# One weight unit of the output projection passed through the ring of the input weights, two padding tiles taken out, and an output group kept in PSUM

## The chip, the core and the metric

The kernel runs on one core of one Trainium2 chip, in one launch. The metric is the device time of that core in microseconds (us). Three runs of the kernel before took 145.35, 144.41 and 146.16 us; their median, 145.35 us, is the time before.

## What is computed

One decoder layer on 256 tokens of width 1024, all in float32:

```python
h = rms_norm(x, norm_pre_g)
q_a,k_a,v_a,g_a,f_a,q_b,k_b,v_b,g_b = split(h @ w_in)      # 16 heads of 64: 8 per group
log_f = log_sigmoid(f_a + fox_forget_b)
y_a = softmax(causal(q_a k_a / 8 + F[t] - F[s])) v_a * silu(g_a)    # F = cumsum(log_f)
y_b = softmax(causal(q_b k_b / 8 - slope * (t - s))) v_b * silu(g_b)
y = concat(y_a, y_b) @ w_out
out = x + rms_norm(y, norm_post_g)
```

With 256 tokens the block-sparse group has one block, so it is plain causal attention with a distance bias.

## The kernel before, in words

**Precision.** Each float32 operand of a large product is written as a high part (rounded to the type fp32r) and a low part (the operand minus the high part), and a product is three passes: high by high, high by low, low by high. ScalarE (ACT) makes the high part of a weight unit (`unit_high`, L385), VectorE (DVE) the low part (`unit_low`, L631), and TensorE (PE) then multiplies. All engines' programs are written out by hand in order; nothing schedules them. An engine goes on only when the semaphores that it waits for have reached their counts.

**The ring of weight units.** `w_in` is cut into units of 128 x 1024 float32 (512 KB). A unit is loaded by SyncE's queue (SP) into one of four slots of `raw`; ACT and DVE write its parts into the slot of the same number in `w_hi` and `w_lo`. Unit u uses slot u % 4. There are 8 value units (0 to 7), 8 gate units (8 to 15), and then 16 that alternate between queries and keys: query 0 is unit 16, key 0 is unit 17, and so on. Three rules tie the engines together. The load of unit u waits until the low part of unit u - 4 is made (semaphore `s_lo`). The high part of unit u waits for its load and until PE has used unit u - 4 (`s_used`). PE waits for `s_lo` before unit u. PE multiplies a gate, query or key unit in 24 matmuls of 256 columns (8 tiles of the inner dimension by three passes, `column_unit`, L942).

**The output weights.** `w_out` is eight units of the same size. Units 4 to 7 pass through the ring at its end. Units 0 to 3 are loaded outside it, into two borrowed buffers (`y_parts` and `gpost_row`), and their parts go to their own tiles `wo_hi` and `wo_lo` (L389 and L706). Two padding tiles of 32 columns lie before and after `w_hi` and `w_lo`; nothing reads them, they only move the addresses of what is allocated behind them.

**Between gates and queries.** While PE multiplies gate units 4 to 7 (units 12 to 15), DVE scales each finished gate out of PSUM (`gate_product`, L695; PE's next unit but one waits for it), makes the low part of the normalised input h in two halves (`normed_low`, L701; PE needs the first half before query 0 and the second halfway through it), and makes the low parts of units 15 to 17. At the same time the decay rows of the forget gates go through a scratch in HBM and come back spread over the partitions: ACT issues that read at L467, 1 MB into `squares`. GpSimd (POOL) then adds the causal mask in four operations (`fox_bias`, L333 and L334) that read and write SBUF. ACT makes the high parts, applies SiLU to all gates (L516, which needs all eight gate products and a table load before it), and then copies each query and key out of PSUM (L508, L512).

**The row of inverse norms.** Before the last value unit PE needs 1/rms of every token along the free dimension: DVE writes two 128 x 128 diagonal matrices (L666, into the buffer `bias`), and PE multiplies them by a tile of ones (L999) in plain float32. The result is `rrow`, which all gate products use.

**The tail.** The output rows are five groups in PSUM: columns 0 to 511 and 512 to 1023 of the first 128 tokens, columns 0 to 511 of the second (group 2), and two of 256 columns (groups 3 and 4). For each, ACT squares and sums it, DVE multiplies it by `norm_post_g` (`times_g`, L897) and, when the row's norm is known, adds it to x (`residual`, L903). Group 3 is left in PSUM by `times_g`; the others are written to `y_post` in SBUF (the profile calls that buffer `h`). Of group 4 ACT scales the columns (L613) and POOL adds x (L373), and the last store waits for that.

## Time and profile before

| | us |
|---|---|
| median of three runs | 145.35 |
| the profiled execution, as timed | 144.79 |
| its span, first to last instruction | 143.0 |
| TensorE matmul busy | 134.6 (94%) |
| VectorE busy | 109.1 (76%) |
| ScalarE busy | 97.0 (68%) |
| GpSimd busy | 39.6 (28%) |

The profile is of one execution; 1.8 us of its time lie outside the span. Busy shares are averages over stages with different limits. Matmuls are pipelined, so a matmul that "took" 0.28 us may start every 0.113 us; the start times say how fast PE goes. A start time is counted from the first instruction.

### The profile page before, as it was taken

The numbers are of one execution on the slowest core, as the hardware profiler recorded it, in microseconds if no ns is written. First come the engines' busy times: TensorE is split into PE (matmuls) and PEld (weight loads), VectorE is DVE, ScalarE is ACT, GpSimd is POOL, SyncE is SP. The second block draws the span as 40 slices with busy tenths as digits, with TensorE's granted clock in tenths as the row PEclk, the third lists the DMA queues.
The fourth block names the chain that finished last, engine by engine and source line by source line (L and its number), as shares of the span: only waits on it lengthen the run. The fifth ranks groups of instructions, "written<-read, shape, count | busy, mean of one in ns | idle before, by whom it ended". The sixth has DMA issues, their size and how long they took to land.

```text
span 143.0 us, 2849 instructions
## 1 busy us (share of the span) xinstructions
PE 134.6 (94%) x1076; PEld 127.1 (89%) x1076; DVE 109.1 (76%) x224; ACT 97.0 (68%) x199; POOL 39.6 (28%) x58
## 2 busy tenths in 40 slices
PE   7889999999999999999999999999999999999920
PEld 7778999999999999999999999999998888988920
DVE  0457967899999799888898995999679825571790
ACT  4557988269955469886884977788879823341850
POOL 3522100000000088000399417040655460220002
PEclk9999999999999999999999999999999999999996
DMA  4899999789565998866467704447800000000034
GB/s 99 252 280 385 401 395 378 236 272 376 178 181 188 419 384 244 307 198 180 132 215 249 251 5 151 147 147 249 343 5 0 0 5 0 0 0 0 0 147 149
DMA packets 9725, 26.96 MB, mean 189 GB/s; under 512 B 1384, under 2 KB 2416, under 8 KB 9456
## 3 DMA queue, kind: packets, MB, share of 16 engines
q1 hardware_dynamic: 9120, 25.57, 51.7%
q10 hardware_dynamic: 592, 1.22, 2.2%
q8 instruction: 8, 0.13, 0.4%
q14 instruction: 5, 0.04, 0.1%
HBM read 25.73 MB, written 1.06 MB: 187 GB/s over the span
## 4 chain that ended last, share of the span: by engine, by line
PE 85%; DMA 4%; DVE 3%; ACT 2%; SPq 2%; issue 1%; POOLq 1%; ACTq 0%
PE bank L942 47%; PE score_banks L952 10%; PE bank L1133 7%; PE score_banks L1133 5%; PE score_banks L1038 4%; DMA raw<-in_w_units 4%; PE value_banks L952 4%; PE value_banks L1049 1%; PE value_banks L1061 1%; PE value_banks L1065 1%; PE value_banks L1050 1%; SPq L221 1%; DVE x_t L903 1%; ACT squares L600 1%; PE bank L1051 1%
## 5 line engine op out<-in xcount | busy, mean ns | idle before, releaser
L631 DVE TENSOR_TENSOR w_lo<-raw,w_hi 128x1024 fp32r<-128x1024 f32 (+1 forms) x33 | 44.7, 1358 | 4.4 <-ACT w_hi L385 4.2
L385 ACT ACTIVATE w_hi<-raw 128x1024 fp32r<-128x1024 f32 (+1 forms) x33 | 34.8, 1057 | 6.0 <-PE bank L942 3.3
L942 PE MATMUL bank<-h_hi,w_hi 128*128 128x256 f32 x128 | 35.8, 280 | 0.0
L942 PE MATMUL bank<-h_lo,w_hi 128*128 128x256 f32 x128 | 35.4, 276 | 0.0
L942 PE MATMUL bank<-h_hi,w_lo 128*128 128x256 f32 x128 | 35.4, 276 | 0.0
L942 PEld LDWEIGHTS bank<-h_hi,w_hi 128*128 128x128 f32 x128 | 24.0, 188 | 0.4
L942 PEld LDWEIGHTS bank<-h_lo,w_hi 128*128 128x128 f32 x128 | 24.0, 188 | 0.0
L942 PEld LDWEIGHTS bank<-h_hi,w_lo 128*128 128x128 f32 x128 | 24.0, 188 | 0.0
L341 POOL TENSOR_TENSOR probs<-probs,row_inv 128x256 f32<-128x256 f32 (+1 forms) x16 | 15.7, 1006 | 27.9 <-DVE row_inv L779 27.8
L942 PE MATMUL bank<-xg_hi,w_hi 128*128 128x256 f32 x64 | 17.9, 279 | 0.0
L942 PE MATMUL bank<-xg_lo,w_hi 128*128 128x256 f32 x64 | 17.8, 278 | 0.0
L942 PE MATMUL bank<-xg_hi,w_lo 128*128 128x256 f32 x64 | 17.8, 278 | 0.0
L333 POOL TENSOR_TENSOR bias<-squares,causal 128x256 f32<-128x256 f32 x4 | 6.3, 1572 | 34.7 <-DMA squares<-decay_rows_scratch 34.7
L481 ACT ACTIVATE probs<-probs,neg_max 128x128 f32<-128x128 f32 (+1 forms) x32 | 14.1, 448 | 0.6 <-DVE neg_max L772 0.6
L942 PEld LDWEIGHTS bank<-xg_hi,w_hi 128*128 128x128 f32 x64 | 12.0, 188 | 0.0
L942 PEld LDWEIGHTS bank<-xg_hi,w_lo 128*128 128x128 f32 x64 | 12.0, 188 | 0.0
L942 PEld LDWEIGHTS bank<-xg_lo,w_hi 128*128 128x128 f32 x64 | 12.0, 188 | 0.0
L952 PE MATMUL score_banks<-w_hi,xg_hi 128*128 128x512 f32 (+2 forms) x34 | 9.0, 341 | 1.2 <-ACT w_hi L415 1.1
L952 PE MATMUL score_banks<-w_lo,xg_hi 128*128 128x512 f32 (+2 forms) x34 | 8.6, 328 | 0.0
L952 PE MATMUL score_banks<-w_hi,xg_lo 128*128 128x512 f32 (+2 forms) x34 | 8.6, 328 | 0.0
L346 POOL TENSOR_TENSOR xg_lo<-y_parts,xg_hi 128x512 fp32r<-128x512 f32 x3 | 5.3, 1773 | 11.2 <-ACT xg_hi L492 11.2
L952 PEld LDWEIGHTS score_banks<-w_hi,xg_hi 128*128 128x128 f32 x34 | 5.8, 188 | 2.3 <-issue 1.1
(167 smaller groups left out, 323.2 us busy)
## 6 DMA issues: line engine op xcount, KB each, us to landing
raw<-in_w_units SPq DMA_DIRECT2D x30, 512.0 KB, 4.3
raw<-in_w_out SPq DMA_DIRECT2D x4, 512.0 KB, 3.3
h<-in_x SPq DMA_DIRECT2D x2, 512.0 KB, 7.1
y_parts<-in_w_out SPq DMA_DIRECT2D x2, 512.0 KB, 5.7
gpost_row<-in_w_out SPq DMA_DIRECT2D x2, 512.0 KB, 4.9
squares<-decay_rows_scratch ACTq DMA_DIRECT2D x1, 1024.0 KB, 5.7
x_t<-in_x SPq DMA_DIRECT2D x1, 1024.0 KB, 7.4
raw<-in_w_units SPq DMA_DIRECT2D x3, 256.0 KB, 4.2
```

The lines of the kernel that those rows point to most:

```text
L221: sp.dma_start(raw[:, u % RING, lo:hi].rearrange("p (a c) -> p a c", a=n), w_units[units, :, part][0:n].rearrange("a p c -> p a c")).then_ ...
L333: pool.tensor_tensor(bias[:, own, :], decay[:, heads, 0:P], mask, ALU.add).then_inc(s_bias, 1)
L341: pool.tensor_tensor(own, own, row_inv[:, 4 * b + t:4 * b + 4:2].unsqueeze(2).to_broadcast((P, 2, hi - lo)), ALU.mult).then_inc(s_norm, 1)
L346: pool.tensor_tensor(y[1][:, 2 * d:2 * d + 2, :], y32[:, :, :], y[0][:, 2 * d:2 * d + 2, :].bitcast(F32), ALU.subtract).then_inc(s_ylo, 1)
L385: nc.scalar.activation(w[0][:, s, 0:width], raw[:, s, 0:width], ACT.Copy).then_inc(s_hi, 1)
L481: nc.scalar.activation(own, own, ACT.Exp, bias=neg_max[:, c:c + 1], scale=-1.0, accum_out=row_sum[:, c:c + 1]).then_inc(s_exp, 1)
L600: nc.scalar.activation(junk[:, t, cols], group, ACT.Square, accum_out=out_sq[:, n:n + 1]).then_inc(s_osq, 1)
L631: nc.vector.tensor_tensor(w[1][:, s, 0:width], raw[:, s, 0:width], w[0][:, s, 0:width].bitcast(F32), ALU.subtract).then_inc(s_lo, 1)
L942: last = nc.tensor.matmul(dst, stationary(a, j), moving(b, j), start=n == 1, stop=n == count * len(PASSES))
L952: last = nc.tensor.matmul(v_banks[t][c][:, lo - first:hi - first], xg[a][:, u, t * P:(t + 1) * P], w[b][:, u % RING, lo:hi], start=u == 0 ...
L1038: last = nc.tensor.matmul(s_ps[:, 2 * (i % 2) + a, lo:hi], q[x][own, i % 4, t * P:(t + 1) * P], k[z][own, i % 2, 0:hi - lo], start=n == 0, ...
L1133: last = nc.tensor.matmul(dst, y[a][:, p, t * P:(t + 1) * P], wide, start=p == 0 and (a, b) == PASSES[0], stop=p == PAIRS - 1 and (a, b) = ...
```

## The change

Six edits, all in one diff.

1. The two padding tiles beside `w_hi` and `w_lo` are gone, so those two lie 128 bytes per partition lower.
2. Output unit 0 is now ring unit 16, in slot 0, between the gates and the queries. Its parts go straight to `wo_hi` and `wo_lo`. Query 0 becomes unit 17 in slot 1, key 0 unit 18 in slot 2, and so on: keys take even slots. Outside the ring only output units 1 to 3 are left.
3. ACT no longer makes the high part of output unit 0 before the forget gates' exponential, but after unit 15; DVE makes its low part between the products of gates 5 and 6, and makes the low parts of query 0 and key 0 one after the other after the second half of h.
4. Since the slot of query 1 is now that of gate 7, its high part waits for gate 7 (before, for gate 6).
5. The diagonal matrices are made in two parts, in the key buffers `k_hi` and `k_lo`, and PE multiplies them by ones in fp32r, in two matmuls of 256 columns. POOL writes one more tile of ones.
6. `times_g` leaves group 2 in PSUM too, and `residual` reads it from there.

```diff
-        sb("ring_shift", [P, RING_SHIFT])
         w = [sb(f"w_{n}", [P, RING, V_PITCH], F32R) for n in PARTS]
-        sb("ring_shift_back", [P, RING_SHIFT])
...
-UNITS = V_UNITS + G_UNITS + QK_UNITS
-QK_0 = V_UNITS + G_UNITS
+OUT_IN_RING = V_UNITS + G_UNITS
+QK_0 = OUT_IN_RING + 1
+UNITS = QK_0 + QK_UNITS
...
-OUT_BEHIND = (V_UNITS + 3, V_UNITS + 5, V_UNITS + 11, V_UNITS + 13)
+OUT_BEHIND = (V_UNITS + 5, V_UNITS + 11, V_UNITS + 13)
...
-                if j > 1:
-                    sp.wait_ge(s_olo, j - 1)
+                if j == 3:
+                    sp.wait_ge(s_olo, 1)
...
-            out_unit_high(0)
...
-            unit_high(0, 80, V_UNITS + 5)
+            act.wait_ge(s_raw_in[0], 80)
+            nc.scalar.activation(wo[0][:, 0, :], raw[:, 0, 0:UNIT], ACT.Copy).then_inc(s_hi, 1)
...
-                unit_high(u % RING, 16 * (u // RING + 1), u + 1 - RING)
+                used = u + 1 - RING if u - RING < OUT_IN_RING else u - RING
+                unit_high(u % RING, 16 * (u // RING + 1), used)
...
+            next_high(key_unit(0))
             next_high(query_unit(1))
...
             for t in range(TT):
-                nc.vector.tensor_scalar(diag[:, t, :], ident[:, :], rstd[:, t:t + 1], None, ALU.mult).then_inc(s_diag, 1)
+                nc.vector.tensor_scalar(diag[0][:, t, :], ident[:, :], rstd[:, t:t + 1], None, ALU.mult).then_inc(s_dhigh, 1)
+            for t in range(TT):
+                dve.wait_ge(s_dhigh, t + 1)
+                nc.vector.scalar_tensor_tensor(out=diag[1][:, t, :], in0=ident[:, :], scalar=rstd[:, t:t + 1],
+                                               in1=diag[0][:, t, :].bitcast(F32), op0=ALU.mult,
+                                               op1=ALU.subtract).then_inc(s_diag, 1)
...
-            out_unit_low(0)
             unit_low(2, 15)
             gate_product(V_UNITS + 4)
             normed_low(0)
             unit_low(3, 16)
             gate_product(V_UNITS + 5)
-            unit_low(0, 17)
+            dve.wait_ge(s_hi, OUT_IN_RING + 1)
+            nc.vector.tensor_tensor(wo[1][:, 0, :], raw[:, 0, 0:UNIT], wo[0][:, 0, :].bitcast(F32),
+                                    ALU.subtract).then_inc(s_lo, 1)
             gate_product(V_UNITS + 6)
             normed_low(1)
             unit_low(1, 18)
+            unit_low(2, 19)
             gate_product(V_UNITS + 7)
             out_unit_low(1)
...
-                kept = group if n == 3 else y_post[:, t, cols]
+                kept = group if n in KEPT_GROUPS else y_post[:, t, cols]
...
-            for t in range(TT):
-                last = nc.tensor.matmul(rrow_ps[:, t * P:(t + 1) * P], ones[:, :], diag[:, t, :], start=True, stop=True)
+            for n in range(2):
+                last = nc.tensor.matmul(rrow_ps[:, 0:SEQ], ones_parts[:, :], k[n][:, 0, :], start=n == 0, stop=n == 1)
```

**VectorE between the gates and the queries.** Before, from the product of gate 4 on; `w_lo` is the low part of a weight unit (unit 15, then query 0, then key 0), `gate` a gate product, `h_lo` a half of h:

```order
L695 TENSOR_TENSOR gate<-bank,rrow 128x256 [waits unit_used]
L701 TENSOR_TENSOR h_lo<-h,h_hi 128x1024 [waits h_hi]
L631 TENSOR_TENSOR w_lo<-raw,w_hi 128x1024 [waits unit_hi]
L695 TENSOR_TENSOR gate<-bank,rrow 128x256 [waits unit_used]
L631 TENSOR_TENSOR w_lo<-raw,w_hi 128x1024 [waits unit_hi]
L695 TENSOR_TENSOR gate<-bank,rrow 128x256 [waits unit_used]
L701 TENSOR_TENSOR h_lo<-h,h_hi 128x1024 [waits h_hi]
L631 TENSOR_TENSOR w_lo<-raw,w_hi 128x1024 [waits unit_hi]
L695 TENSOR_TENSOR gate<-bank,rrow 128x256 [waits unit_used]
```

And the same place in the changed kernel:

```order
L705 TENSOR_TENSOR gate<-bank,rrow 128x256 [waits unit_used]
L711 TENSOR_TENSOR h_lo<-h,h_hi 128x1024 [waits h_hi]
L636 TENSOR_TENSOR w_lo<-raw,w_hi 128x1024 [waits unit_hi]
L705 TENSOR_TENSOR gate<-bank,rrow 128x256 [waits unit_used]
L755 TENSOR_TENSOR wo_lo<-raw,wo_hi 128x1024 [waits unit_hi]
L705 TENSOR_TENSOR gate<-bank,rrow 128x256 [waits unit_used]
L711 TENSOR_TENSOR h_lo<-h,h_hi 128x1024 [waits h_hi]
L636 TENSOR_TENSOR w_lo<-raw,w_hi 128x1024 [waits unit_hi] x2
L705 TENSOR_TENSOR gate<-bank,rrow 128x256 [waits unit_used]
```

The low part of query 0 has moved from ahead of the product of gate 6 to behind the second half of h; its old place is output unit 0's.

**ScalarE at the same place.** Before, from the store of the decay rows to the first query:

```order
L463 DMA decay_rows_scratch<-probs 8x256 [waits decay_rows]
L385 ACTIVATE w_hi<-raw 128x1024 [waits unit_used,raw_in3]
L385 ACTIVATE w_hi<-raw 128x1024 [waits unit_used,raw_in0]
L467 DMA squares<-decay_rows_scratch 128x2048 [waits decay_stored]
L385 ACTIVATE w_hi<-raw 128x1024 [waits unit_used,raw_in1]
L385 ACTIVATE w_hi<-raw 128x1024 [waits unit_used,raw_in2,constants]
L516 ACT_TABLE_LOAD
L516 ACTIVATE gate<-gate 128x2048 [waits gate_products]
L508 ACTIVATE q_hi<-bank 128x256 [waits unit_used]
```

and changed:

```order
L465 DMA decay_rows_scratch<-probs 8x256 [waits decay_rows]
L388 ACTIVATE w_hi<-raw 128x1024 [waits unit_used,raw_in3]
L468 ACTIVATE wo_hi<-raw 128x1024 [waits raw_in0]
L470 DMA squares<-decay_rows_scratch 128x2048 [waits decay_stored]
L388 ACTIVATE w_hi<-raw 128x1024 [waits unit_used,raw_in1]
L388 ACTIVATE w_hi<-raw 128x1024 [waits unit_used,raw_in2,constants]
L388 ACTIVATE w_hi<-raw 128x1024 [waits unit_used,raw_in3]
L519 ACT_TABLE_LOAD
L519 ACTIVATE gate<-gate 128x2048 [waits gate_products]
L511 ACTIVATE q_hi<-bank 128x256 [waits unit_used]
```

Between the read of the decay rows and the table load there are now three high parts instead of two: query 0, key 0 and query 1, and the last of them waits for gate 7.

## Rows read from the trace of the kernel before

**Rows 1.** The profile's page: busy time by engine, TensorE's granted clock.

```profile
PE 134.6 (94%) x1076; PEld 127.1 (89%) x1076; DVE 109.1 (76%) x224; ACT 97.0 (68%) x199; POOL 39.6 (28%) x58
PEclk9999999999999999999999999999999999999996
```

**Rows 2.** The chain that ended last: shares, then two pieces (start, us, what).

```profile
PE 85%; DMA 4%; DVE 3%; ACT 2%; SPq 2%; issue 1%; POOLq 1%; ACTq 0%
...
26.43 0.45 PE bank L999 x4
...
41.14 24.60 PE bank L942 x216
```

**Rows 3.** L942 by stretch: length, PE busy, PEld busy, clock, DMA share, GB/s.

```profile
35.22:38.04 2.82, 2.82 (x27) 2.82 (x25) 1.00 0.45 151
38.04:40.76 2.72, 2.72 (x26) 2.69 (x24) 1.00 0.64 208
51.98:54.70 2.72, 2.72 (x26) 2.72 (x25) 1.00 0.91 318
```

**Rows 4.** Timeline of PE: start, us, operation, [idle before <-releaser].

```profile
10.29 0.38 PE L952 MATMUL score_banks<-w_hi,xg_hi 128*128 128x256 f32 x1 [0.44 <-ACT w_hi L415]
...
26.15 0.28 PE L952 MATMUL value_banks<-w_lo,xg_hi 128*128 128x264 f32 x1
26.27 0.61 PE L999 MATMUL bank<-bias,ones 128*128 128x128 f32 x4
26.63 0.48 PE L952 MATMUL score_banks<-w_hi,xg_hi 128*128 128x512 f32 x1
```

**Rows 5.** Timeline of DVE at the diagonal matrices.

```profile
23.65 0.48 DVE L666 TENSOR_SCALAR bias<-ident,rstd 128x128 f32<-128x128 f32 x2
```

**Rows 6.** Timeline of DVE from unit 16's low part to key 0's.

```profile
47.31 1.20 DVE L631 TENSOR_TENSOR w_lo<-raw,w_hi 128x1024 fp32r<-128x1024 f32 x1
49.46 0.42 DVE L695 TENSOR_TENSOR gate<-bank,rrow 128x256 f32<-128x256 f32 x1 [0.94 <-PE bank L942]
49.80 1.22 DVE L701 TENSOR_TENSOR h_lo<-h,h_hi 128x1024 fp32r<-128x1024 f32 x1
50.93 1.76 DVE L631 TENSOR_TENSOR w_lo<-raw,w_hi 128x1024 fp32r<-128x1024 f32 x1
52.62 0.41 DVE L695 TENSOR_TENSOR gate<-bank,rrow 128x256 f32<-128x256 f32 x1
...
58.82 0.41 DVE L794 TENSOR_TENSOR k_lo<-bank,k_hi 128x256 fp32r<-128x256 f32 x1
```

**Rows 7.** Timeline of POOL: the first two mask operations.

```profile
50.47 1.14 POOL L333 TENSOR_TENSOR bias<-squares,causal 128x256 f32<-128x256 f32 x1 [34.66 <-DMA squares<-decay_rows_scratch]
51.57 1.73 POOL L334 TENSOR_TENSOR squares<-squares,causal 128x256 f32<-128x256 f32 x1
```

**Rows 8.** Timeline of ACT from the read of the decay rows to query 0's copy.

```profile
44.65 0.35 ACTq L467 DMA_DIRECT2D squares<-decay_rows_scratch  x1
49.54 1.07 ACT L385 ACTIVATE w_hi<-raw 128x1024 fp32r<-128x1024 f32 x1 [1.68 <-PE bank L942]
50.62 1.28 ACT L516 ACT_TABLE_LOAD   x1
54.90 0.39 ACT L508 ACTIVATE q_hi<-bank 128x256 fp32r<-128x256 f32 x1
```

**Rows 9.** DMA issues from 47.1 us: names, size, us to landing (unit 19).

```profile
raw<-in_w_units SPq DMA_DIRECT2D x1, 512.0 KB, 6.0
```

**Rows 10.** Timelines of DVE, ACT and POOL at the end, then the chain there.

```profile
138.35 0.75 DVE L903 SCALAR_TENSOR_TENSOR x_t<-h,rstd,x_t 128x512 f32<-128x512 f32 x1
...
138.41 0.51 ACT L613 ACTIVATE h<-h,rstd 128x256 f32<-128x256 f32 x1 [0.54 <-DVE rstd L915]
...
139.42 0.72 POOL L373 TENSOR_TENSOR x_t<-x_t,h 128x256 f32<-128x256 f32 x1 [11.09 <-ACT h L613]
...
138.97 0.42 issue
```

More of the change, by code:

```diff
@@ L58 @@
 WARM_UP = 8
-N_CONST = 3
+N_CONST = 4
+KEPT_GROUPS = (2, 3)
 PASSES = ((0, 0), (0, 1), (1, 0))
@@ L106, in hybrid_layer @@
         ones = sb("ones", [P, P])
+        ones_parts = sb("ones_for_parts", [P, P], F32R)
         causal = sb("causal", [P, P])
@@ L125, in hybrid_layer @@
         y = xg
-        diag = bias[:, 0:TT, :]
+        diag = [k[n][:, 0, :].rearrange("p (t c) -> p t c", t=TT) for n in range(2)]
         y32, y_cross = y_parts[:, 0:2, :], y_parts[:, 2:4, :]
@@ L237, in load_unit @@
                 sp.wait_ge(s_lo, r * RING + s + 1 - RING)
-                sp.dma_start(raw[:, s, 0:UNIT], w_units[r * RING + s]).then_inc(s_raw_in[s], 16)
+                u = r * RING + s
+                src = w_out[0] if u == OUT_IN_RING else w_units[u if u < OUT_IN_RING else u - 1]
+                sp.dma_start(raw[:, s, 0:UNIT], src).then_inc(s_raw_in[s], 16)
             def load_out_unit(j):
-                if j > 1:
-                    sp.wait_ge(s_olo, j - 1)
+                if j == 3:
+                    sp.wait_ge(s_olo, 1)
                 sp.dma_start(raw_out[j % 2], w_out[j]).then_inc(s_raw_out_in[j % 2], 16)
@@ L257, in _ @@
                 if u in OUT_BEHIND:
-                    load_out_unit(OUT_BEHIND.index(u))
+                    load_out_unit(OUT_BEHIND.index(u) + 1)
             for i in range(1, PAIRS + 1):
@@ L302, in _ @@
             pool.memset(eps_col[:, :], EPS).then_inc(s_const, 1)
+            pool.memset(ones_parts[:, :].bitcast(F32), 1.0).then_inc(s_const, 1)
             pool.wait_ge(s_wf_in, 16)
@@ L387, in out_unit_high @@
             def out_unit_high(j):
[L388 removed]
+                act.wait_ge(s_raw_out_in[j % 2], 16 * ((j + 1) // 2))
                 nc.scalar.activation(wo[0][:, j, :], raw_out[j % 2], ACT.Copy).then_inc(s_ohi, 1)
@@ L504, in query_high @@
             def query_high(i):
-                act.wait_ge(s_used, QK_0 + 1 + 2 * i)
+                act.wait_ge(s_used, QK_0 + 2 * i)
                 scale = 1.0 if i < FOX_PAIRS else q_scale[:, i - FOX_PAIRS:i - FOX_PAIRS + 1]
@@ L510, in key_high @@
             def key_high(i):
-                act.wait_ge(s_used, QK_0 + 2 + 2 * i)
+                act.wait_ge(s_used, QK_0 + 1 + 2 * i)
                 nc.scalar.activation(k[0][:, i % 2, :], bank[k_bank[i]][:, 0:SEQ], ACT.Copy).then_inc(s_khi, 1)
@@ L555, in _ @@
             next_high(key_unit(5))
-            act.wait_ge(s_olo, OUT_OWN)
+            act.wait_ge(s_olo, OUT_OWN - 1)
             for d in range(1, QUADS - 1):
@@ L704, in out_unit_low @@
             def out_unit_low(j):
-                dve.wait_ge(s_ohi, j + 1)
+                dve.wait_ge(s_ohi, j)
                 nc.vector.tensor_tensor(wo[1][:, j, :], raw_out[j % 2], wo[0][:, j, :].bitcast(F32),
@@ L901, in residual @@
                 cols = out_groups[groups - 1][1]
-                kept = out_groups[3][2] if groups == 4 else y_post[:, t, cols]
+                kept = out_groups[groups - 1][2] if groups - 1 in KEPT_GROUPS else y_post[:, t, cols]
                 nc.vector.scalar_tensor_tensor(out=x_nat[:, t, cols], in0=kept, scalar=rstd[:, t:t + 1],
@@ L1070, in query @@
                 pe.wait_ge(s_lo, QK_0 + 1 + 2 * i)
-                column_unit(bank[q_bank[i]], 2 * (i % 2), h, halfway)
+                column_unit(bank[q_bank[i]], (QK_0 + 2 * i) % RING, h, halfway)
             def key(i):
                 pe.wait_ge(s_lo, QK_0 + 2 + 2 * i)
-                column_unit(bank[k_bank[i]], 2 * (i % 2) + 1, h)
+                column_unit(bank[k_bank[i]], (QK_0 + 1 + 2 * i) % RING, h)
             pe.wait_ge(s_hlo, 1)
@@ L1131, in out_part @@
                     for a, b in PASSES:
-                        wide = wo[b][:, p, cols] if p < OUT_OWN else w[b][:, p - OUT_OWN, cols]
+                        wide = wo[b][:, p, cols] if p < OUT_OWN else w[b][:, (UNITS + p - OUT_OWN) % RING, cols]
                         last = nc.tensor.matmul(dst, y[a][:, p, t * P:(t + 1) * P], wide,
@@ L1141, in _ @@
             scores(7)
-            pe.wait_ge(s_olo, OUT_OWN)
+            pe.wait_ge(s_olo, OUT_OWN - 1)
             pe.wait_ge(s_ylo, 1)
```

7 lines of the change are left out of this document (3 added, 4 removed).

## The prediction, made before the changed kernel was timed

> **What bounds the kernel now.** I read the page first, for the engines' shares and the clock [rows 1]. The reader is to see TensorE (PE) busy for 94% of the span, and its granted clock at full speed (2.4 GHz) in every slice but the last. Next I read the chain of waits [rows 2]: 85% of it is PE, and from 41.14 us it runs through 216 matmuls of L942 with no other engine between them. So a microsecond counts only if PE starts later or sooner for it, or if it lies in the tail behind PE's last matmul. VectorE (DVE), ScalarE (ACT) and GpSimd (POOL) matter where PE reaches a wait before they are done. Then I read PE's speed by unit [rows 3]: a query, key or gate unit of 24 matmuls takes 2.72 us, and some gate units 2.82 us at the same clock. Last come the timelines of DVE, POOL and ACT around 50 us, where the change moves work [rows 6 to 8], and of the tail [rows 10].
>
> **The diagonal matrices (edit 5).** Before, PE's two float32 products at L999 appear as four records between 26.27 and 26.63 us, 0.36 us by their starts, and the 512-column matmul behind them takes 0.48 us [rows 4]; the chain of waits puts 0.45 us on the four [rows 2], with the slow start of what follows. Now there are two matmuls of 256 columns in fp32r; at 2.72 / 24 = 0.113 us each [rows 3] that is 0.23 us. If the slower matmul behind them stays, 0.36 - 0.23 = 0.13 us is gained; if it goes, 0.45 - 0.23 = 0.22. I take 0.21, because the operand type no longer changes there. DVE pays for two more 128-column operations, about 0.2 us each by the start at 23.65 and the next at 24.05 [rows 5], plus a short wait. The matrices are then ready at about 24.6 us, and PE asks for them at 26.1, so this costs nothing. The low part of value unit 7 is 0.45 us later, and PE asks for it only in the last of that unit's three passes, while DVE starts it first thing. POOL's extra memset lies in its idle time at the start.
>
> **Output unit 0 in the ring, and its work moved (edits 2 and 3).** ACT and DVE make as many parts as before, and the loads are as many bytes. DVE's 1.1 us for the low part of output unit 0 at 42 us moves to 47 us, where before the low part of query 0 ran, and then DVE idled 0.94 us for gate 6 [rows 6]. What matters is what was pushed back: the low part of query 0 now follows gate 6's product and the second half of h. Step by step, with everything on PE 0.21 us earlier: DVE starts gate 6's product at 49.46 - 0.21 = 49.25 us, the second half of h at 49.59, the low part of query 0 at 50.72. Before, the operation that started at this place (50.93) took 1.76 us, although the same operation took 1.20 at 47.31 [rows 6]. The difference is POOL's masks: the first starts at 50.47 when the decay rows land, and they and DVE's operations alternate, one waiting for the other (the second mask takes 1.73 us) [rows 7]. So query 0's low part ends at 50.72 + 1.76 = 52.48 us. PE has finished gate 7 at 51.98 - 0.21 = 51.77 [rows 3] and waits 0.71 us. A matmul that starts after a wait takes 0.38 us against 0.28 [rows 4], which is 0.10 more. PE then goes on at 52.58 against 51.98: **0.60 us later than before**, the 0.21 us gained at the diagonal already taken off.
>
> The bounds of this step: if the decay rows land after 50.72, DVE goes first, the low part takes 1.22, ends at 51.94, and PE is 0.06 us later than before. If they land a microsecond sooner, one more mask runs ahead, and DVE is later by at most another 0.5 us (1.76 less 1.20, with rounding): PE is 1.1 us later. The read is issued after the same store, and the load before it starts a little sooner now, so I take the value of the trace and keep the upper bound.
>
> **The slots moved by one (edits 2 and 4).** Query 1's high part, issued at 49.54 us before [rows 8], now waits for gate 7 (51.77, with ACT's start 0.28 us behind) and for its load. That unit 19 was loaded from 47.1 us on and took 6.0 us to land, beside the decay rows and an output unit [rows 9]; by that row it would land at 52.9 at the latest, by the smaller traffic before it at 52. So ACT starts it at 52.05 to 52.9. Behind it come the table load and SiLU, and then query 0's copy. From the high part's start to the table load is 1.08 us, the load takes 1.28, and SiLU was followed by the copy at 54.90; the copy now comes at 56.3 to 57.1, 1.4 to 2.2 us later than before [rows 8]. PE wants it for query 1, at 52.58 + 2 x 2.72 = 58.0 us, so that is met. The same delay runs on to key 0's low part, which key 1 waits for: before, it was done at 59.23 [rows 6], and key 1 began at 51.98 + 3 x 2.72 = 60.14 us, 0.91 us later. Against a PE that is 0.60 later, the chain is 0.8 to 1.6 us later; it has that 0.91 and some idle time on ACT to give. What is left is a second wait of 0 to 0.5 us; I take 0.15. From there on each engine does the same work in the same order, with slot numbers changed only. The third direct output unit's load holds SP's queue until the first one's low part is made, about 56 us; the loads behind it run four units ahead of PE, 11 us at 2.72 us a unit, so I cost this at nothing; without that lead it would be one landing time more.
>
> **Group 2 kept in PSUM (edit 6).** At the end ACT has scaled the last columns at 138.92 us, but POOL starts its addition only at 139.42; the chain calls 0.42 us of that "issue" [rows 10]. In this time DVE runs the residual of group 2, which reads two SBUF buffers, until 139.10. A DVE operation that reads PSUM and one SBUF buffer was not slowed while POOL ran: the gate product took 0.41 at 52.62 and 0.42 at 49.46 [rows 6, 7]. With group 2 in PSUM the residual is of that kind. I therefore take the 0.42 us off, between 0 (POOL was held by something else) and 0.42. The Trainium skill says the same (SBUF — State Buffer, Who interferes with whom): a VectorE instruction with at most one SBUF input does not contend with GpSimd, one with two does. By that rule the sum keeps the 0.42; without it, it would be 0.42 us worse, which is the fourth rival. POOL's addition would then end at 138.97 + 0.72 = 139.69 us and, with the store behind it, still be the last work.
>
> **The padding (edit 1).** No row shows what an address costs. The nearest are the two speeds of PE, 2.82 and 2.72 us a unit [rows 3], which change at unit borders with no wait. I take 0, because slots 0 to 3 all run at 2.72 from query 0 on. The bounds are the rivals below. The Trainium skill has it that only the port pair of VectorE and GpSimd is contended and that TensorE never waits on anyone (SBUF — State Buffer, Who interferes with whom). By that the two rivals on PE's speed would have no chance at all; the two speeds in this trace, which it does not explain, keep me from giving them none.
>
> **The sum.** 0.60 + 0.15 - 0.42 = +0.33 us. On the profiled execution, 144.79, that gives 145.1; it stands 0.56 us below the median of the three runs, so the median to expect is 145.35 + 0.33 = **145.7 us**.
>
> **The rivals.**
> - *No wait for query 0.* The masks come after the low part. PE is 0.06 later, the tail 0.42 shorter: 145.0 us. For it: the landing needs to slip by only 0.3 us. Against it: one load fewer runs beside that read.
> - *Slower: PE falls to its other speed.* If query and key units at the new addresses take 2.82 us, 16 x 0.10 = 1.6 us are added: 147.3 us. It is slower than the time before from four such units on. For it: two speeds exist, unexplained. Against it: the speed changed between units without any address changing.
> - *Faster: more of PE gets the better speed.* The eight value units and four of the gate units, at 0.10 each, give 1.2 us back: 144.5 us; together with no wait for query 0, 143.8.
> - *The change does not do what it says in the tail*, because POOL's 0.42 us is its own start, and the second wait is at its upper end: 0.60 + 0.5 = +1.1 us, 146.45 us.
>
> **How the numbers follow.** The forecast gets 0.54, no wait 0.12, PE slower 0.13, PE faster 0.10, the fourth 0.11. The runs of the kernel before differ by 1.2%, so about 1% is what can be told from no change: 143.90 and 146.80 are the borders. Slower by more: the second rival, and a part of the fourth with the runs' spread, 0.16. Faster by more: half of the third and a little spread, 0.10. Between: 0.74. The range of 144.2 to 147.0 us holds the forecast, the first, the fourth and most of the third, and leaves out most of the second.
>
> **What would show it.** Right: in the profile of the changed kernel PE idles once near 52 us, released by the low part of a weight unit, for 0.5 to 0.9 us; the value unit behind the row of norms starts about 0.2 us sooner; POOL's last addition starts within 0.1 us of ACT's last operation; L942 keeps 2.72 us a unit. Wrong: no idle PE there; POOL's last start still 0.4 us late; a second wait above 0.5 us before key 1 or later; units of 2.82 us among queries and keys.

## The result, and the profile after

The changed kernel takes **146.28 us** (median of 14 runs, 144.67 to 149.67) beside 144.98 for the kernel before (14 runs): a ratio of 1.0075, 95% interval 1.005 to 1.0101. Timed again with the experiments it read 146.53 us (6 runs, 145.02 to 148.33), ratio 1.0128 (1.0089 to 1.0168) to 144.65. The ratios and intervals here and below leave out executions more than 1.5% above the fastest of the same kernel, so for a kernel whose times scatter they lie below the quotient of the medians, which is 1.0090 in the first timing. So it is about 1% slower, on the border of what counts as a change. The median lies 0.6 us above the forecast of 145.7 us and inside its range (144.2 to 147.0). That it is so near is partly luck: the time before was taken from three runs (145.35), where 14 give 144.98. The change itself was forecast at +0.33 us and measured at +1.30, and the terms of the sum are further off than the total.

The profile below is that of the second timing (145.02 us, span 143.2, the lowest of its runs; the kernel before was profiled at 144.79 us). The profiled execution of the first timing took 149.67 us, the highest of its runs, and is read by itself at the end of this section. First the page: busy time, TensorE's clock, and the shares of the chain of waits, against [rows 1, 2]:

```profile
PE 134.6 (94%) x1074; PEld 126.9 (89%) x1074; DVE 109.2 (76%) x226; ACT 96.9 (68%) x199; POOL 39.6 (28%) x59
...
PEclk9999999999999999999999999999999999999996
...
PE 50%; DVE 21%; DMA 14%; ACT 7%; SPq 3%; issue 2%; POOLq 1%; ACTq 0%
```

PE does the same work at the same clock. What changed is the chain of waits, the last of these lines: PE has 50% of it, not 85%. The chain itself shows why (start, us, what):

```profile
45.66 6.72 DMA raw<-in_w_units
52.40 1.06 ACT w_hi L388
...
54.77 1.92 ACT gate L519
56.96 0.95 ACT w_hi L388
57.94 1.23 DVE w_lo L636
59.16 1.14 DVE wo_lo L716
60.69 5.73 PE bank L954 x48
```

Until 60.69 us the end is not set by PE. It goes from the load of unit 19, which holds query 1, to ACT, DVE and only then to PE; before, 216 matmuls stood there with nothing between them. Before, unit 19 was key 1's: it was issued at about 47.1 us [rows 9], 2.4 us behind the read of the decay rows, and the last high part ahead of the table load was unit 18's, which waited for PE and not for a load [rows 8]. Now unit 19's high part stands in that place, and its load is issued at 45.66 us, 1.3 us behind the read (44.40). Read PE's timeline at the places that the prediction names (start, us, operation, idle before; L954 is L942 of before, L1012 is L999):

```profile
25.76 0.28 PE L1012 MATMUL bank<-k_hi,ones_for_parts 128*128 128x256 f32 x1
...
26.00 0.74 PE L964 MATMUL score_banks<-w_hi,xg_hi 128*128 128x512 f32 x3
...
51.16 0.36 PE L954 MATMUL bank<-h_hi,w_hi 128*128 128x256 f32 x1 [0.16 <-DVE w_lo L636]
...
57.47 0.39 PE L954 MATMUL bank<-h_hi,w_hi 128*128 128x256 f32 x1 [0.52 <-DVE q_lo L797]
...
60.69 0.39 PE L954 MATMUL bank<-h_hi,w_hi 128*128 128x256 f32 x1
```

The last matmuls ahead of these three start at 50.73, 56.67 and 60.29, so their starts are 0.43, 0.80 and 0.40 us apart where 0.11 is usual. That makes three waits of 0.32, 0.69 and 0.29 us, 1.30 in all, at query 0, query 1 and key 1. DVE, POOL and ACT around them:

```profile
49.79 2.89 DVE L636 TENSOR_TENSOR w_lo<-raw,w_hi 128x1024 fp32r<-128x1024 f32 x2
...
56.99 0.42 DVE L797 TENSOR_TENSOR q_lo<-bank,q_hi 128x256 fp32r<-128x256 f32 x1 [0.94 <-ACT q_hi L511]
...
50.23 1.38 POOL L336 TENSOR_TENSOR bias<-squares,causal 128x256 f32<-128x256 f32 x1 [34.50 <-DMA squares<-decay_rows_scratch]
...
52.40 1.06 ACT L388 ACTIVATE w_hi<-raw 128x1024 fp32r<-128x1024 f32 x1 [2.93 <-DMA raw<-in_w_units]
53.48 1.28 ACT L519 ACT_TABLE_LOAD   x1
54.77 1.92 ACT L519 ACTIVATE gate<-gate 128x2048 f32<-128x2048 f32 x1
56.60 0.36 ACT L511 ACTIVATE q_hi<-bank 128x256 fp32r<-128x256 f32 x1
```

DVE's query 0 low part is the first of the two at 49.79. It starts before the first mask (50.23), and PE goes on at 51.16, 1.37 us after its start: it took its quick 1.2 us, not 1.76. ACT stands idle for 2.93 us until unit 19 has landed, and the table load, SiLU and query 0's copy are queued behind it. PE's pace by unit (length, PE busy, PEld busy, clock), against [rows 3]:

```profile
28.82:31.54 2.72, 2.72 (x24) 2.72 (x25) 1.00 0.72 203
...
51.16:53.95 2.79, 2.79 (x23) 2.79 (x24) 1.00 1.01 404
57.47:60.29 2.82, 2.82 (x24) 2.82 (x24) 1.00 0.97 327
```

The first gate units are quick now; queries 0 and 1 are slow. And the tail, against [rows 10]:

```profile
139.03 0.75 DVE L915 SCALAR_TENSOR_TENSOR x_t<-bank,rstd,x_t 128x512 f32<-128x512 f32 x1
...
139.09 0.51 ACT L618 ACTIVATE h<-h,rstd 128x256 f32<-128x256 f32 x1 [0.54 <-DVE rstd L927]
...
139.74 0.72 POOL L376 TENSOR_TENSOR x_t<-x_t,h 128x256 f32<-128x256 f32 x1 [10.73 <-ACT h L618]
```

POOL starts 0.14 us after ACT has ended (139.60), against 0.50 before.

**The difference of the two spans, piece by piece.** From the span's start to the row products PE is 0.51 us sooner (25.76 against 26.27), though its program there is the same. In the profiles of ten other runs these products start anywhere from 25.94 to 26.64 us (and at 28.65 in one more), so most of this is spread. From them to gate 0 3.06 us instead of 3.29: -0.23. From gate 0 to query 0 22.34 against 22.42: -0.08, in which three quick gates cancel the wait. From query 0 to the output product (110.44, against 109.76) 59.28 against 57.78: **+1.50**. Of that, 0.98 are the waits at query 1 and key 1; the other 0.5 is that query 0, query 1 and key 1 take 2.91, 2.93 and 2.85 us from their first matmul on, and not 2.72. From PE's last matmul (137.20, against 136.52) to the end 6.03 against 6.45: -0.42. The sum is +0.26 by these rounded positions, which is the 0.2 us between the spans.

**The execution at the other end.** In the profile of the first timing, unit 19 was late. Its DMA issue (size, us to landing), 6.7 us in the other profile and 6.0 before [rows 9]:

```profile
raw<-in_w_units SPq DMA_DIRECT2D x1, 512.0 KB, 8.9
```

The timelines of PE and ACT, and the stretch behind query 1's start (length, PE busy, PEld busy, clock):

```profile
59.73 0.58 PE L954 MATMUL bank<-h_hi,w_hi 128*128 128x256 f32 x1 [2.60 <-DVE q_lo L797]
...
54.66 1.06 ACT L388 ACTIVATE w_hi<-raw 128x1024 fp32r<-128x1024 f32 x1 [5.02 <-DMA raw<-in_w_units]
```

```profile
59.70:66.50 6.80, 6.77 (x34) 6.77 (x35) 0.54 0.53 178
```

PE stood for 2.8 us before query 1 (56.85 to 59.73, less 0.11), and behind that its granted clock was at half (1.2 GHz of 2.4) until about 65.9 us: the 34 matmuls of the stretch took 6.80 us where 34 x 0.113 = 3.85 is usual, 2.95 us more. So the wait is 2.1 us longer than in the other profile (0.69), key 1 waits 0.3 less, and the clock adds 2.95: about 4.75 us, where the two times differ by 4.65. The Trainium skill (TensorE: Matmul & The Clock Gate, What's actually happening) says that the slower clock is the default and that activity lifts it; the granted clock behind this stop (0.54 over the stretch) agrees.

### The profile page after: what moved, and what is told of

It reads as the page before. It is cut to its first block, busy times and chain, and to the rows that moved or that the text cites. A ratio compares the mean times of both kernels' runs of the same rounds, so it can differ in the third digit from the quotient of the medians.

```text
span 147.9 us, 2849 instructions
## 1 busy us (share of the span) xinstructions
PE 137.3 (93%) x1074; PEld 129.8 (88%) x1074; DVE 108.4 (73%) x226; ACT 96.9 (65%) x199; POOL 37.0 (25%) x59
## 4 chain that ended last, share of the span: by engine, by line
PE 52%; DVE 19%; DMA 15%; ACT 4%; issue 4%; SPq 3%; POOLq 1%; ACTq 0%
PE bank L954 28%; DMA raw<-in_w_units 10%; PE bank L1146 7%; DVE w_lo L636 6%; PE score_banks L1146 5%; DMA h<-in_x 5%; PE score_banks L1051 4%; DVE h L684 2%; DVE v L698 2%; SPq L221 2%; PE value_banks L1062 1%; PE value_banks L1074 1%; PE value_banks L1078 1%; DVE gate L705 1%; PE value_banks L1063 1%
## 5 line engine op out<-in xcount | busy, mean ns | idle before, releaser
L636 DVE TENSOR_TENSOR w_lo<-raw,w_hi 128x1024 fp32r<-128x1024 f32 (+1 forms) x33 | 43.4, 1321 | 7.4 <-ACT w_hi L388 7.3
L954 PE MATMUL bank<-h_hi,w_hi 128*128 128x256 f32 x128 | 37.5, 293 | 2.8 <-DVE q_lo L797 2.6
L954 PE MATMUL bank<-h_lo,w_hi 128*128 128x256 f32 x128 | 36.7, 287 | 0.0
L954 PE MATMUL bank<-h_hi,w_lo 128*128 128x256 f32 x128 | 36.6, 286 | 0.0
L954 PEld LDWEIGHTS bank<-h_hi,w_hi 128*128 128x128 f32 x128 | 25.4, 198 | 3.5 <-DVE q_lo L797 2.8
L954 PEld LDWEIGHTS bank<-h_lo,w_hi 128*128 128x128 f32 x128 | 25.5, 199 | 0.0
L954 PEld LDWEIGHTS bank<-h_hi,w_lo 128*128 128x128 f32 x128 | 25.4, 198 | 0.0
L954 PE MATMUL bank<-xg_hi,w_hi 128*128 128x256 f32 x64 | 17.8, 278 | 0.0
L954 PE MATMUL bank<-xg_lo,w_hi 128*128 128x256 f32 x64 | 17.7, 276 | 0.0
L954 PE MATMUL bank<-xg_hi,w_lo 128*128 128x256 f32 x64 | 17.7, 276 | 0.0
L336 POOL TENSOR_TENSOR bias<-squares,causal 128x256 f32<-128x256 f32 x4 | 5.1, 1278 | 36.2 <-DMA squares<-decay_rows_scratch 36.2
L954 PEld LDWEIGHTS bank<-xg_hi,w_hi 128*128 128x128 f32 x64 | 12.0, 188 | 0.0
L954 PEld LDWEIGHTS bank<-xg_lo,w_hi 128*128 128x128 f32 x64 | 12.0, 188 | 0.0
L954 PEld LDWEIGHTS bank<-xg_hi,w_lo 128*128 128x128 f32 x64 | 12.0, 188 | 0.0
```

The source lines that it names most:

```text
L336: pool.tensor_tensor(bias[:, own, :], decay[:, heads, 0:P], mask, ALU.add).then_inc(s_bias, 1)
L636: nc.vector.tensor_tensor(w[1][:, s, 0:width], raw[:, s, 0:width], w[0][:, s, 0:width].bitcast(F32), ALU.subtract).then_inc(s_lo, 1)
L954: last = nc.tensor.matmul(dst, stationary(a, j), moving(b, j), start=n == 1, stop=n == count * len(PASSES))
```

## The experiments

All were timed in five rounds, each beside the kernel before on the same chip. The last three ran on another chip than the rest; the kernel before read 144.66 us there, and 144.65 and 144.75 on the first.

**The changed kernel again** (no edit; its profile is the one above).

> The changed kernel once more, unchanged. Theory L (late load): TensorE's wait is not at query 0 but at query 1, because query 1's weight unit (unit 19) lands behind the 1 MB read of the decay rows and an output unit; ScalarE then starts the table load and SiLU late and copies query 0 late. It expects unit 19 to land after 53 us, an idle TensorE of 0.5 to 2.5 us just before query 1, and a time of 145.5 to 147 us. Theory M (masks, the step of the prediction): TensorE waits 0.7 us for the low part of query 0, which GpSimd's masks delay, and less than 0.5 us at query 1 or key 1. It expects the longest idle of TensorE at query 0, near 51.8 us.

146.53 us, ratio 1.0128 (1.0089 to 1.0168): slower, with three waits, as read above. The longest is at query 1, as theory L has it and theory M does not, though unit 19 landed at 52.38 us, sooner than the 53 that L expected.

**A small read of the decay rows.** The read of the decay rows, 1 MB, is cut to 128 KB; the masks of the other heads are computed from data that is not theirs, so the output differs.

```diff
-act.dma_start(decay[:, :, :], decay_dram.partition_broadcast(P))
+act.dma_start(decay[:, 0:1, :], decay_dram[0:1, :].partition_broadcast(P))
```

> The changed kernel with the read of the decay rows cut from all eight heads (1 MB) to one head (128 KB); this leaves out the decay rows of seven heads, whose places hold other numbers, so the attention of group A is not the reference's. All operations stay. Theory L expects unit 19 to land by 51.5 us, SiLU to start about 54.5 us, no idle TensorE at query 1, and 1 to 2 us less than the changed kernel. Theory M expects the masks to start some 3 us sooner, near 47.5 us, and to be over before query 0's low part; the wait at query 0 would go too, but it is 0.7 us at most, so at most 0.7 us less.

144.88 us (12 runs), ratio 1.0021 (0.9995 to 1.0048): 1.65 us less than the changed kernel, where M allowed 0.7 at most. The loss against the kernel before is gone. Timelines of PE, ACT, DVE and POOL:

```profile
52.06 0.36 PE L954 MATMUL bank<-h_hi,w_hi 128*128 128x256 f32 x1 [0.80 <-DVE w_lo L636]
...
51.89 1.06 ACT L388 ACTIVATE w_hi<-raw 128x1024 fp32r<-128x1024 f32 x1 [2.17 <-DMA raw<-in_w_units]
...
50.16 3.44 DVE L636 TENSOR_TENSOR w_lo<-raw,w_hi 128x1024 fp32r<-128x1024 f32 x2
...
48.41 0.74 POOL L336 TENSOR_TENSOR bias<-squares,causal 128x256 f32<-128x256 f32 x1 [32.20 <-DMA squares<-decay_rows_scratch]
```

Two things come out. POOL starts on the decay rows 1.8 us sooner (48.41, for 50.23), the masks then do run beside query 0's low part (the first of the two at 50.16), and PE waits 0.96 us there (its last matmul at 50.99, the next at 52.06): the mechanism of the prediction, between its value (0.71) and its upper bound, 0.5 us more. And there is no wait at query 1 or key 1. Unit 19 landed after 5.7 us. The longest wait at query 0 of all these kernels goes with a time 1.65 us lower than the first experiment's. So a wait at query 0 does not add to one at query 1: as far as PE would have had to wait there anyway, it takes that one's place. What is longer than that is paid, here 0.73 us by the figures under "DVE's order alone".

**The tail alone** (the kernel before, with group 2 kept in PSUM).

```diff
+KEPT_GROUPS = (2, 3)
-kept = group if n == 3 else y_post[:, t, cols]
+kept = group if n in KEPT_GROUPS else y_post[:, t, cols]
```

> The kernel before with edit 6 alone: output group 2 stays in PSUM. If the port of VectorE and GpSimd held the last addition back, it now starts within 0.1 us of the end of ScalarE's last scaling and the time is 0.42 us less than before (ratio 0.997). If GpSimd's start is late for a reason of its own, the addition still starts 0.4 us late and the time is that of before.

144.56 us, ratio 0.9994 (0.9974 to 1.0013). ACT, then POOL:

```profile
138.07 0.51 ACT L614 ACTIVATE h<-h,rstd 128x256 f32<-128x256 f32 x1 [0.54 <-DVE rstd L916]
...
139.08 0.72 POOL L374 TENSOR_TENSOR x_t<-x_t,h 128x256 f32<-128x256 f32 x1 [11.09 <-ACT h L614]
```

POOL still starts 0.50 us after ACT ends (138.58). Edit 6 by itself is worth nothing that can be told.

**The diagonal matrices alone** (the kernel before, with edit 5).

```diff
-    last = nc.tensor.matmul(rrow_ps[:, t * P:(t + 1) * P], ones[:, :], diag[:, t, :], start=True, stop=True)
+    last = nc.tensor.matmul(rrow_ps[:, 0:SEQ], ones_parts[:, :], k[n][:, 0, :], start=n == 0, stop=n == 1)
```

> The kernel before with edit 5 alone: the diagonal matrices in two parts, multiplied in fp32r. Forecast: the two products take 0.23 us, and the matmul behind them starts 0.13 to 0.22 us sooner than at 26.63 us; the time is 0.2 us less than before (ratio 0.9985). The rival is that switching to the tile of ones written by GpSimd, or the later low part of value unit 7, costs as much as is won: no difference in the time, and TensorE's start of the first gate unit stays at 29.56 us.

143.85 us, ratio **0.9934** (0.9911 to 0.9957), the fastest of all. PE, ACT and POOL:

```profile
26.64 0.28 PE L1007 MATMUL bank<-k_hi,ones_for_parts 128*128 128x256 f32 x1
...
138.54 0.51 ACT L615 ACTIVATE h<-h,rstd 128x256 f32<-128x256 f32 x1 [0.54 <-DVE rstd L922]
...
139.19 0.72 POOL L375 TENSOR_TENSOR x_t<-x_t,h 128x256 f32<-128x256 f32 x1 [10.73 <-ACT h L615]
```

From the products to gate 0 (29.68) it is 3.04 us instead of 3.29 (-0.25), and POOL's last addition comes 0.14 us after ACT's end instead of 0.50, with group 2 not in PSUM. The two together, 0.61 us, explain why the ratio is lower than the 0.9985 expected. Of POOL's program this edit changes one thing: there is one memset more, at the start.

**One more instruction on POOL** (the kernel before, with a memset of a tile that nobody reads).

```diff
+spare = sb("spare", [P, 1])
 pool.memset(eps_col[:, :], EPS).then_inc(s_const, 1)
+pool.memset(spare[:, :], 1.0)
```

> The kernel before with one more small memset on GpSimd at its start, into a tile that nothing reads, and nothing else. Keeping group 2 in PSUM did not start GpSimd's last addition sooner, while the kernel with the two-part diagonal, whose GpSimd program is one instruction longer, did. Theory P (position in GpSimd's program): the addition starts 0.1 us after its wait is over instead of 0.46, and the time is 0.35 us less. Theory D (something of the diagonal itself, such as the buffer it no longer uses): the addition still starts 0.46 us after, and the time is that of before.

144.24 us, ratio **0.995** (0.9922 to 0.9978). ACT and POOL:

```profile
138.26 0.51 ACT L615 ACTIVATE h<-h,rstd 128x256 f32<-128x256 f32 x1 [0.54 <-DVE rstd L917]
...
138.91 0.72 POOL L375 TENSOR_TENSOR x_t<-x_t,h 128x256 f32<-128x256 f32 x1 [10.72 <-ACT h L615]
```

0.14 us again. Theory P holds and D does not: one instruction more at the start of POOL's program takes 0.36 us off its last start, 138 us later. Why it does is not shown.

**The padding alone** (the kernel before, without the two tiles).

```diff
-sb("ring_shift", [P, RING_SHIFT])
-sb("ring_shift_back", [P, RING_SHIFT])
```

> The kernel before with edit 1 alone: the two padding tiles taken out. In the changed kernel gate units 0 to 2 ran at 113 ns a matmul instead of 118, and queries 0 and 1 at 118 instead of 113. If addresses set this, gate units 0 to 2 take 2.72 us each here instead of 2.82 and the time is about 0.3 us less, unless some query or key units (those in odd slots, as in the changed kernel) become slow, at 0.1 us each; with eight of them slow it is 0.5 us more. If the order of loads and conversions sets it, the units keep the speeds of the kernel before and the time does not change.

144.78 us, ratio 1.0005 (0.9971 to 1.0039). Two units of PE (columns as above):

```profile
29.36:32.08 2.72, 2.72 (x24) 2.72 (x25) 1.00 0.77 286
66.63:69.45 2.82, 2.82 (x23) 2.82 (x24) 1.00 0.55 174
```

Gates 0 to 2 and 4 leave the slow pace, and six of the later units take it up. The layout does change which units are slow; the net is nothing.

**The diagonal matrices without the padding** (the kernel before, with edits 5 and 1: the two diffs above together).

> The kernel before with edits 5 and 1: two-part diagonal and no padding, the ring as it was. The diagonal alone gave a ratio of 0.9934. If the padding's removal gives gate units 0 to 2 their better speed and costs nothing elsewhere, the ratio is 0.991; if odd slots become slow for keys, it is 0.997 or worse.

143.92 us, ratio 0.9946 (0.9915 to 0.9976), not to be told from the diagonal matrices alone.

**Both orders put back.** The changed kernel, with the low part of query 0 ahead of gate 6's product (DVE), and the SiLU and query 0's copy ahead of query 1's parts (ACT, and the low parts on DVE to match).

```diff
+unit_low(1, 18)
 gate_product(V_UNITS + 6)
 normed_low(1)
-unit_low(1, 18)
...
-next_high(query_unit(1))
 gates_silu()
 query_high(0)
+next_high(query_unit(1))
...
-next_low(query_unit(1))
 query_low(0)
+next_low(query_unit(1))
```

> The changed kernel with two reorderings: VectorE makes the low part of query 0 before gate 6's product, in its idle time there, and ScalarE applies SiLU and copies query 0 before it makes the high part of query 1 (VectorE likewise takes query 0's low part of the copy first). Theory L: TensorE no longer waits at query 0; query 1 waits only for its own load and parts, about 54 + 1.1 + 1.2 us at the earliest against 56.5, so 0 to 0.8 us in all; the time falls by 1 to 1.8 us, to that of the kernel before or up to 0.5 us less, and no run has a clock at half speed before the tail. If the loads are late for every reader alike, nothing is won at query 1 and only the 0.4 us at query 0.

144.81 us (12 runs, 144.06 to 146.84), ratio 0.9992 (0.996 to 1.0024). The profile is of the execution at 146.84 us. PE early on, and at query 1:

```profile
8.64 0.39 PE L964 MATMUL score_banks<-w_hi,xg_hi 128*128 128x256 f32 x1 [1.88 <-ACT w_hi L418]
...
59.39 0.36 PE L954 MATMUL bank<-h_hi,w_hi 128*128 128x256 f32 x1
```

There is no wait at query 0, 0.23 us is left at query 1 (59.05 to 59.39, less 0.11) and 0.04 at key 1. What makes this execution long lies ahead of all that: ACT waits 2.74 us for one of the first loads, PE stands for it until 8.64 us, the granted clock is 0.70 from 10.0 to 14.5 us, and the first gate starts at 31.71 us, 2.15 later than before. So the expectation that no execution has the half clock ahead of the tail failed, and a load near the start is a second source of scatter, which has nothing to do with the orders. The two orders together are worth 1.4% against the changed kernel's second timing and 0.8% against its first: the whole loss against the kernel before. The time does not fall to the 0.9946 of edits 5 and 1 alone; the two intervals overlap, and what the unit in the ring may still cost is not taken apart. The next two runs take the orders apart.

**DVE's order alone** (the first hunk).

> The changed kernel with one line moved on DVE: the low part of query 0 runs ahead of gate 6's product and of the second half of h, at the place it had before the change. ACT's order stays as changed, so query 1's high part still waits for unit 19's load ahead of the table load and the SiLU. The changed kernel read 1.0128 times before when it was run again, with 0.44 us between PE's matmul starts at query 0 (0.33 more than the usual 0.11), 0.80 at query 1 and 0.40 at key 1. Theory S (the waits are separate costs and add up): the one at query 0 goes (-0.3 us), those at query 1 and key 1 stay at 0.7 and 0.3 us, ratio about 1.010. Rival L (the load alone sets when query 1 can start; what is not waited for at query 0 is waited for later): the wait at query 0 goes and comes back whole at query 1, 1.0 to 1.1 us there, ratio 1.012 to 1.013.

147.13 us (6 runs, 145.24 to 150.21), ratio 1.0093 (1.0057 to 1.0129), against 1.0128; the quotient of its medians is 1.017. PE at query 1 and ACT at its high part, then the stretch behind (columns as above), and the load's landing:

```profile
59.00 0.39 PE L954 MATMUL bank<-h_hi,w_hi 128*128 128x256 f32 x1 [2.17 <-DVE q_lo L797]
...
53.94 1.06 ACT L388 ACTIVATE w_hi<-raw 128x1024 fp32r<-128x1024 f32 x1 [4.08 <-DMA raw<-in_w_units]
```

```profile
59.00:63.47 4.47, 4.47 (x25) 4.47 (x25) 0.62 0.61 215
```

```profile
raw<-in_w_units SPq DMA_DIRECT2D x1, 512.0 KB, 7.9
```

The wait at query 0 is gone, and nothing is won by that. The interval holds what both theories expected, 1.010 and 1.012 to 1.013, and the wait at query 1, 2.33 us, is longer than either expected. What speaks for L is how it follows the landing. In three executions now ACT has this order and PE is held at query 1. Unit 19 landed in them at 52.38, 53.91 and 54.64 us (issued at 45.66, 45.99 and 45.78, with the landing times shown), and query 1's first matmul started at 57.47, 59.00 and 59.73: **5.09 us later each time**, with a wait at query 0 and without. With the small read the load landed at 51.87, which would release PE at 56.96; PE came there at 57.69, after two units behind 52.06, and did not wait. It was 0.73 us later than the load asked for, and by these positions that is the part of its 0.96 us at query 0 that cost time (an estimate).

**ACT's order alone** (the other two hunks).

> The changed kernel with ACT's order changed: the table load, the SiLU and query 0's copy run ahead of query 1's high part, which waits for the late load of unit 19 (DVE's two low parts change places in the same way). DVE's order around query 0 stays as changed. Both orders together read 0.9992 times before. Theory L (ACT standing still for the late load, with the table load, the SiLU and query 0's copy behind it, makes the waits at query 1 and key 1): those fall from 0.80 and 0.40 us to 0.1 to 0.3 each, the wait at query 0 stays at 0.3 to 1.0 us, ratio about 1.003 to 1.006. Rival D (the order on DVE around query 0 was what mattered): the waits at query 1 and key 1 stay, ratio 1.011 to 1.013.

144.88 us (12 runs, 144.43 to 145.88), ratio 1.0017 (0.9998 to 1.0036). Timelines of ACT, DVE and PE:

```profile
53.33 1.93 ACT L519 ACTIVATE gate<-gate 128x2048 f32<-128x2048 f32 x1 [2.29 <-DVE gate L705]
55.16 0.36 ACT L511 ACTIVATE q_hi<-bank 128x256 fp32r<-128x256 f32 x1
...
50.07 2.89 DVE L636 TENSOR_TENSOR w_lo<-raw,w_hi 128x1024 fp32r<-128x1024 f32 x2
52.89 0.41 DVE L705 TENSOR_TENSOR gate<-bank,rrow 128x256 f32<-128x256 f32 x1
...
57.88 0.36 PE L954 MATMUL bank<-h_hi,w_hi 128*128 128x256 f32 x1 [0.76 <-DVE w_lo L636]
```

```profile
57.88:60.60 2.72, 2.72 (x24) 2.72 (x25) 1.00 0.93 309
```

The interval takes in the low end of what L expected (1.003 to 1.006) and rules D (1.011 to 1.013) out. Yet L was not right about the waits. That at key 1 is gone, and the runs scatter less. At query 1 PE still waits 0.93 us (56.84 to 57.88, less 0.11), where L expected 0.1 to 0.3. The load has nothing to do with it: it had landed at 52.6, and ACT turned to it only after query 0's copy at 55.16. What holds PE now is that DVE makes two low parts (2.89 us, with the masks between) ahead of gate 7's product, for which the SiLU waits 2.29 us. With DVE's order put back as well, 0.23 us of it is left. So DVE's new order makes a wait behind ACT's old one, and none that shows in the changed kernel, where what hangs on the load ends later still. The last row is the stretch of query 1 (columns as above).

**Both orders back, and the padding too.**

```diff
+sb("ring_shift", [P, 32])
 w = [sb(f"w_{n}", [P, RING, V_PITCH], F32R) for n in PARTS]
+sb("ring_shift_back", [P, 32])
```

> The changed kernel with both orders put back and the 128 bytes of padding before the weight parts put back too (and behind them), so that the weight slots have the addresses they had before the change. Theory A (addresses set the speed of a unit): gates 0 to 2 run at 117.7 ns a matmul again as before the change (+0.32 us) and the units from query 1 to query 2, which ran at 117.6 without the padding, run at 113.3 (-0.3 us); ratio equal to that without the padding (0.9992) within 0.003. Rival U (the unit's speed goes with the slot and the unit's rank, not with the address): the speeds of all units stay as in the kernel without the padding.

145.75 us (9 runs: eight from 144.75 to 146.68, and one of 173.57 at a mean clock of 0.76, which has no profile), ratio 1.0064 (1.0029 to 1.0099): the padding, put back, costs 0.7%. Both theories miss that. Of the 24 gate, query and key units twelve are slow here; these are gate 0 and key 1:

```profile
29.57:32.39 2.82, 2.82 (x24) 2.82 (x25) 1.00 0.67 198
60.74:63.56 2.82, 2.82 (x25) 2.82 (x24) 1.00 0.77 248
```

By the same count (a middle interval of 118 ns between starts instead of 113) it is 4 before, 6 without the padding, 3 with both orders back, 2 in the changed kernel, and none with ACT's order alone. Nine more than without the padding, at 0.10 us each, are 0.9 us, and the two medians differ by 145.75 - 144.81 = 0.94. So theory A is right that addresses set the pace (gates 0 to 2 are slow again) and wrong on the rest: queries and keys did not gain. And the address alone isn't the rule. Query 1 has the same addresses with both orders back as with ACT's alone; its middle interval is 118 ns in the one and 113 in the other, at the full clock in both.

## Why the prediction was right in its range and wrong in its terms

- **Diagonal matrices: right.** -0.21 forecast, -0.23 and -0.25 measured between the row products and gate 0.
- **The wait at query 0: right mechanism, wrong case, and not a term of the sum.** 0.71 us + 0.10 for the restart was forecast. The decay rows landed at 50.1 us, the first mask came after the low part had begun, and PE waited 0.32 us, near the lower bound of the step (51.94 - 51.77 = 0.17). This is the first rival, to which the prediction gave 0.12. A wait above the forecast one showed with the small read, 0.96 us, in a kernel that was faster all the same.
- **The second wait: the step that failed.** The prediction put it at 0.15 us (0 to 0.5) before key 1, and held it met at query 1. It used one landing time, 6.0 us, of the profile before [rows 9], and a PE that came to query 1 at 58.0 us. Measured: 0.69 us at query 1 and 0.29 at key 1 with a landing of 6.7 us, and 2.8 us at query 1, with a half clock behind it, with 8.9. The chain was followed rightly (ACT's high part, table load, SiLU, copy), and it takes 5.09 us from the landing to PE. With the prediction's own window for the landing, 52.05 to 52.9 us, that is 57.1 to 58.0: the wait was met with 0 to 0.9 us to spare, and less at the upper end than any of PE's terms could be off. In the profile at 145.02 us the landing (52.38) and the copy (56.60) came inside the forecast windows, and what was wrong was PE: it was there at 56.78, 1.2 us sooner than forecast, by its sooner start, the shorter wait at query 0 and the quick gates. In the executions at 147.64 and 149.67 us it was the landing too (53.91 and 54.64 us). What was missed is that a landing time became a term of the path, one for one, where before ACT had nothing to wait for but PE in that place: its spread goes into the kernel's time.
- **The tail: right size, wrong cause.** -0.42 was forecast and -0.42 measured between PE's last matmul and the end. But group 2 in PSUM does nothing (0.9994), and one more POOL instruction does it (0.995). The rule cited, on SBUF inputs of VectorE, was not what held POOL: the residual with one buffer in PSUM took 0.75 us, as the one with both in SBUF did [rows 10]. The residual ended as POOL began (139.78, 139.74), so the rule itself was not put to the test. The rival that had POOL's 0.42 as "its own start" was right about the cause, and so wrong to leave the time there, as another edit took it away.
- **The padding: right at 0 net, wrong in the reason.** "Slots 0 to 3 all run at 2.72 from query 0 on" does not carry over to other addresses: which units are slow changed with the layout, and in one layout with the waits. The prediction's "slower than the time before from four such units on" does not fit its own sum, which lies above that time with none. The rivals on PE's speed (16 slow units, or the better pace for all) came out in neither full form: two units slow instead of four, a gain of 0.2 us.

The forecast's terms were +0.60, +0.15 and -0.42, in sum +0.33; the medians of 14 runs differ by +1.30. Measured in the profile at 145.02 us, between the row products and query 0 -0.31, from there to the output product +1.50, and the tail -0.42: +0.77 us, of which that execution's sooner start hides 0.51. The other runs of the changed kernel lie higher, at medians of 146.28 and 146.53. That unit 19 landed later in them, as in the executions at 147.64 and 149.67 us, is likely: the scatter goes with ACT's order and with the size of the read. It isn't shown run by run, as only profiled executions have a landing time, and the execution at 146.84 us with both orders back was long for another reason.

Of the signs named ahead of the run: the idle PE near 52 us came, shorter; the value unit sooner by 0.2 us and POOL's last start came; the second wait above 0.5 us and units of 2.82 us among the queries, named as what would prove it wrong, came too.

## What to carry to other kernels

A part that is moved behind a load on an in-order engine makes that load's landing time, with its spread, a term of the path: take the landing from several loads under the same traffic, not from one, and put the instructions that wait for nothing ahead of the one that waits for it. Two waits on the same path are not added where the second is for a chain that does not pass through the first: the second shrinks by what the first took. Where several edits are made together, time the small ones alone: here the diagonal matrices by themselves (0.9934) beat both kernels, and the rest of the change gave that back and 1% more.

## What the runs showed of the hardware that was not expected

- **A late load beside a broadcast read.** The 1 MB read of the decay rows and the 512 KB load of unit 19, issued 1.3 to 1.4 us behind it, landed after 5.7 and 6.7 us, 7.5 and 8.9 us, and 8.1 and 7.9 us in the three executions in which PE was held at query 1. With the read cut to 128 KB the load took 5.7.
- **GpSimd's last start.** From ACT's end to POOL's last addition it is 0.50 us in the three kernels with the old program on POOL (before, tail alone, padding alone), and 0.13 to 0.14 us in the ten profiles with one memset more at its start, whatever else they change.
- **Two paces of TensorE at the same clock.** A 256-column matmul starts every 113 or every 118 ns, for whole units. Mostly the slow pace begins behind a break (a wait, other products), but in the profile of the diagonal matrices without the padding key 1 takes it up with none. The layout of the buffers has a part in where it begins, but not alone; the cause is open.
- **What a late load costs twice.** In the two executions in which PE stood still for 2.33 and 2.77 us before query 1, the granted clock was at half behind the stop for some microseconds, which cost 1.75 us more (24 matmuls in 4.47 us, for 2.72; the row counts key 1's first too) and 2.95 us. In a third, 1.88 us of idle PE near the start had a granted clock of 0.50 behind it, between 9.5 and 10.5 us. The stops of 0.3 to 1.0 us between gates and keys had the full clock behind them.
